# Two groups of modulation sums made beside the delta projections, and half a group in each merge round

## The reference

```
proj = rmsnorm(x) @ w_in                       # 12,560 columns
o1 = gated_delta_rule(silu(conv4(qkv)), ...)   # 8 heads of 128, chunks of 64 tokens
o2 = sliding_window_attention(...)             # 8 heads of 64
o3 = stick_breaking_attention(...)             # 4 heads of 128
merged = sum_i sigmoid(gates_i) * (o_i @ w_br_i)
h = x + merged @ w_o
h = h + cross_attention(rmsnorm(h), mem)
h = h + (silu(gate) * val) @ w_down            # gate, val = conv3(rmsnorm(h) @ w_up)
```

```
mod = silu(c) @ mod_w + mod_b                  # [2048] @ [2048, 12288]
sh1, sc1, g1, sh2, sc2, g2 = split(mod, 6)
h = rms_norm(x) * (1 + sc1) + sh1
a, gt = split(h @ conv_w_in + conv_b_in, 2);  u = a * sigmoid(gt)
u = depthwise_conv(u, 31 taps);  u = silu(layer_norm(u)) @ conv_w_out + conv_b_out
x = x + (1 + g1) * u
h = rms_norm(x) * (1 + sc2) + sh2
x = x + (1 + g2) * (square(relu(h @ mlp_w1)) @ mlp_w2)
```

## Time and profile before

| | us |
|---|---|
| median of 3 runs | 2745.66 (2744.92 to 2746.29) |
| the profiled execution's own time | 2738.4 |
| its span, first to last instruction | 2736.8 |
| TensorE busy | 2660.2 (97%) |
| VectorE busy | 1836.4 (67%) |
| ScalarE busy | 1184.8 (43%) |
| mean granted TensorE clock | 0.988 of full speed |

### The profile page before, as it was taken

One profiled execution on the slowest core, in us unless ns is written; L12 is line 12 of the kernel. 1 busy time (PEld: TensorE's weight loads), 2 busy tenths in 40 slices (PEclk: granted clock), 3 DMA queues, 4 the chain that ended last, 5 costly groups with the idle time before them and its releaser, 6 DMA issues.

```text
span 2736.8 us, 46369 instructions
## 1 busy us (share of the span) xinstructions
PE 2660.2 (97%) x18056; PEld 2472.7 (90%) x18056; DVE 1836.4 (67%) x2116; ACT 1184.8 (43%) x1443; POOL 80.4 (3%) x172
## 2 busy tenths in 40 slices
PE   7999999999999998999999989998989999999998
PEld 6999998999998887998899878897889898898997
DVE  4675647788778877776577646998665555555554
ACT  5544426533334455554344452115454334343342
POOL 1000000000010000000000000000000000000000
PEclk9999999999999999999999999999999999999999
DMA  5633435888989875776677644442555665656654
GB/s 185 178 116 101 131 96 194 306 292 303 331 310 317 289 258 191 267 238 226 192 262 241 223 130 131 146 154 93 185 157 185 194 183 188 192 181 191 187 184 153
DMA packets 269373, 553.10 MB, mean 202 GB/s; under 512 B 17026, under 2 KB 54963, under 8 KB 267955
## 3 DMA queue, kind: packets, MB, share of 16 engines
q1 hardware_dynamic: 249698, 442.06, 49.8%
q0 software_dynamic: 18720, 102.77, 11.2%
q10 hardware_dynamic: 816, 6.29, 0.6%
HBM read 548.96 MB, written 2.10 MB: 201 GB/s over the span
## 4 chain that ended last, share of the span: by engine, by line
PE 86%; DVE 8%; ACT 2%; issue 1%; DMA 1%; SPq 0%; POOLq 0%; ACTq 0%; DVEq 0%
PE sums L617 78%; DVE cv L1632 3%; PE small L1487 3%; DVE w_lo L573 1%; DMA mod_raw<-in_mod_w_dram 1%; DVE mod_acc L1177 1%; ACT w_hi L564 1%; PE small L1189 1%; PE small L1608 1%; PE sums L1223 0%; PE small L738 0%; SPq L1686 0%; PE small L1500 0%; PE small L1494 0%; PE small L698 0%
## 5 line engine op out<-in xcount | busy, mean ns | idle before, releaser
L573 DVE TENSOR_TENSOR w_lo<-raw,w_hi 128x1024 fp32r<-128x1024 f32 x790 | 960.1, 1222 | 740.9 <-ACT w_hi L564 738.3
L564 ACT ACTIVATE w_hi<-raw 128x1024 fp32r<-128x1024 f32 x790 | 834.3, 1059 | 1372.5 <-PE sums L617 1193.1
L617 PE MATMUL sums<-x_hi,w_hi 128*128 128x256 f32 x3728 | 1069.0, 287 | 9.1 <-DVE w_lo L573 3.9
L617 PE MATMUL sums<-x_lo,w_hi 128*128 128x256 f32 x3728 | 1060.5, 284 | 0.0
L617 PE MATMUL sums<-x_hi,w_lo 128*128 128x256 f32 x3728 | 1060.2, 284 | 0.0
L617 PEld LDWEIGHTS sums<-x_hi,w_hi 128*128 128x128 f32 x3728 | 720.8, 193 | 13.8 <-issue 8.5
L617 PEld LDWEIGHTS sums<-x_lo,w_hi 128*128 128x128 f32 x3728 | 721.2, 193 | 1.1 <-issue 0.7
L617 PEld LDWEIGHTS sums<-x_hi,w_lo 128*128 128x128 f32 x3728 | 720.7, 193 | 0.0
L617 PE MATMUL sums<-w_hi,y_hi 128*128 128x512 f32 x928 | 364.2, 392 | 7.0 <-issue 6.4
L617 PE MATMUL sums<-w_lo,y_hi 128*128 128x512 f32 x928 | 363.0, 391 | 0.0
L617 PE MATMUL sums<-w_hi,y_lo 128*128 128x512 f32 x928 | 362.8, 391 | 0.0
(11 more groups left out here) (352 smaller groups left out, 1970.1 us busy)
## 6 DMA issues: line engine op xcount, KB each, us to landing
raw<-in_mlp_w_dram SPq DMA_DIRECT2D x256, 512.0 KB, 3.8
raw<-in_w_in_dram SPq DMA_DIRECT2D x198, 512.0 KB, 4.4
mod_raw<-in_mod_w_dram POOLq DMA_DIRECT2D x128, 768.0 KB, 6.1
raw<-in_w_up_dram SPq DMA_DIRECT2D x128, 512.0 KB, 4.4
raw<-in_w_down_dram SPq DMA_DIRECT2D x64, 512.0 KB, 4.4
raw<-in_conv_w_in_dram SPq DMA_DIRECT2D x128, 256.0 KB, 3.2
raw<-in_w_o_dram SPq DMA_DIRECT2D x32, 512.0 KB, 5.6
raw<-in_conv_w_out_dram SPq DMA_DIRECT2D x32, 512.0 KB, 4.3
```

The lines of the kernel that those rows point to most:

```text
L564: act.activation(w_hi[:, s.slot(k), :], raw[:, s.slot(k), :], ACT.Copy).then_inc(hi_ready, 1)
L573: dve.tensor_tensor(w_lo[:, s.slot(k), :], raw[:, s.slot(k), :], w_hi[:, s.slot(k), :].bitcast(F32), ALU.subtract).then_inc(lo_ready, 1)
L617: mm = pe.matmul(o, l, r, start=first and i == 0, stop=end and i + 1 == len(steps), skip_group_check=True)
```

## The change

Groups 0 and 1, 32 mod units, move out of the merge rounds into the second halves of delta chunks 1 to 7: 4, 4, 4, 5, 5, 5 and 5 units. `rest_units` spreads them over the last four units of a chunk, and where there are five, two stand behind the last. They have buffers of their own (`mod_first`, in the space of the residual `h`, and `acc_first` and `acc_second`, in that of `y_hi` and `y_lo`), and both sums are cleared in chunk 1. POOL's loads start when the first norm is scaled. Group 0's `mod_sum` comes ahead of the last unit before the second delta group and waits for the first group's `y_lo`; a wait for `mod_kept` stands between it and L1494's second turn. Group 1's `mod_sum` stands in `attention_pe`. Merge rounds then make half a group each (3, 3 and 2 units in the first three chunks), and sum it in rounds 1 and 3. The whole units of `conv_in` are now 0, 1, 2, 4, 5 and 6, so the split ones are 3 and 7, and the taps are spread differently.

```diff
-CV_WHOLE = 6
+CV_WHOLE = (0, 1, 2, 4, 5, 6)
...
         def mixer_pe(pe):
-            for g in range(2):
-                yield 7 if g == 0 else 5
-                yield from delta_pe(pe, g)
+            yield 7
+            yield from delta_pe(pe, 0)
+            yield 4
+            pe.wait_ge(y_split, 1)
+            mod_sum(pe, KT, acc=acc_first)
+            yield 1
+            pe.wait_ge(mod_kept, 1)
+            yield from delta_pe(pe, 1)
             yield 4
             yield from attention_pe(pe)
...
             ins.then_inc(win_twice, 1)
-            yield 1
+            mod_sum(pe, 2 * KT, acc=acc_second)
+            yield 1
+            pe.wait_ge(mod_kept, 2)
...
         def mixer_dve(dve, own):
-            for g in range(2):
-                yield 8 if g == 0 else 5
-                yield from delta_dve(dve, own, g)
+            yield 8
+            yield from delta_dve(dve, own, 0)
+            yield 3
+            mod_keep(dve, 0, 1)
+            yield 2
+            yield from delta_dve(dve, own, 1)
...
+            pool.wait_ge(norm_scaled, TT)
+            for m in range(EARLY * KT):
+                if m >= 2:
+                    pool.wait_ge(mod_used, m - 1)
+                q, kt = m // KT, m % KT
+                pool.dma_start(mod_first[m % 2][:, :], mod_w_2[0][kt * P:(kt + 1) * P, q * MOD_W:(q + 1) * MOD_W]).then_inc(
+                    mod_loaded[m % 2], 16)
...
-                    rest_units(dve, s, SLOTS + 4, s.size + SLOTS, beside=beside)
+                    n = 4 * g + m
+                    if n == 1:
+                        clear_mod(dve, acc_first)
+                        clear_mod(dve, acc_second)
+                    first = (0, 0, 4, 8, 12, 17, 22, 27, 32)
+                    rest_units(dve, s, SLOTS + 4, s.size + SLOTS,
+                               lambda j: mod_unit(dve, first[n] + j, (first[n] + j) % KT), first[n + 1] - first[n], beside)
...
-                clear_mod(dve)
-                kt = 0
-                for m, units in enumerate((5, 5, 4, 2, 0, 0)):
+                if i % 2 == 0:
+                    clear_mod(dve)
+                kt = 8 * (i % 2)
+                q = EARLY + i // 2
+                for m, units in enumerate((3, 3, 2, 0, 0, 0)):
...
-                    for k, taps_ahead in zip(range(*ahead(s)), (10, 20, 40, 50, 54, 57, 60, CV_B * TAPS)):
+                    for k, taps_ahead in zip(range(*ahead(s)), (8, 16, 24, 31, 39, 47, 55, CV_B * TAPS)):
```

More of the change, by code:

```diff
@@ L90, in is_whole @@
     def is_whole(self, u):
-        first, chunks, size, count = self.whole
-        return first <= u < first + chunks * size and (u - first) % size < count
+        first, chunks, size, which = self.whole
+        return first <= u < first + chunks * size and (u - first) % size in which
     def whole_ahead(self, u):
-        first, chunks, size, count = self.whole
+        first, chunks, size, which = self.whole
         d = min(max(u - first, 0), chunks * size)
-        return d // size * count + min(d % size, count)
+        return d // size * len(which) + sum(k < d % size for k in which)
 class Spot:
@@ L257, in build_program @@
             win_q = sb("win_q", [P, 4, T], scope=s)
+        with ExitStack() as s:
+            mod_first = [sb(f"mod_first{j}", [P, MOD_W], scope=s) for j in range(2)]
         h = sb("h", [P, TT, D])
@@ L813, in nf_split_dve @@
                     scaled(g + 1)
-                if u == NF_CONV and g < CV_WHOLE:
+                if u == NF_CONV and g in CV_WHOLE:
                     continue
@@ L828, in normed_ready @@
         def normed_ready(pe, u, g):
-            if u == NF_CONV and g < CV_WHOLE:
+            if u == NF_CONV and g in CV_WHOLE:
                 pe.wait_ge(nf_hi, NG * u + g + 1)
             else:
-                pe.wait_ge(nf_split, NF_SPLITS[u] + g + 1 - (CV_WHOLE if u == NF_CONV else 0))
+                pe.wait_ge(nf_split, NF_SPLITS[u] + g + 1 - (sum(k < g for k in CV_WHOLE) if u == NF_CONV else 0))
         def shift1(kt):
@@ L1128, in attention_dve @@
         def attention_dve(dve, own):
+            mod_keep(dve, 1, 2)
             yield 1
@@ L2145, in merge @@
                         beside.rest()
-                    rest_units(dve, s, *ahead(s), lambda j: mod_unit(dve, kt + j, kt + j, (i, KT)), units, beside)
+                    rest_units(dve, s, *ahead(s), lambda j: mod_unit(dve, q * KT + kt + j, kt + j), units, beside)
                     kt += units
@@ L2163, in merge @@
                                   ALU.subtract).then_inc(merged, 1)
-                mod_keep(dve, i, at(1, (i, 1)))
+                if i % 2:
+                    mod_keep(dve, q, q + 1)
             merge(0, beside)
-            with own.loop(4, 3, 1) as i:
+            for i in range(1, 4):
                 merge(i, None)
```

47 lines of the change are left out of this document (25 added, 22 removed).

## The result

The changed kernel takes 2765.22 us (median of 4 executions, 2763.72 to 2771.46), against 2745.97 for the kernel before on the same chip: 1.0072 times as long, 95% interval 1.0057 to 1.0088, which is 16 to 24 us more. I had said 2760.5, in a range of 2750 to 2775. The profiled execution took 2765.18. That is 26.8 more than the profiled one of before, which at 2738.4 was a short one: the kernel before has a median of 2746.2 over 32 executions. So a comparison of the two traces shows some 7 us more than the medians do; I come back to them.

What follows compares the result with a forecast made beforehand. TensorE's chain of matmuls was taken as the bound, busy 2660 of 2737 us. The terms summed to +14.8 on the profiled 2738.4, 2753.2; adding 7.3 to reach the median gave 2760.5, range 2750 to 2775.

Steps and rivals of the forecast that it cites:

- The bound, and the merges: Whole kernel: TensorE's matmul chain bounds it; work taken from merge rounds was hidden, so a round stays at 92.25 us.
- rival C: Delta stage: VectorE's idle time takes in the mod units, only savings remain, 2740.4 us; chance 0.10.
- Term 1: Delta chunks 1 to 3: bursts of mod units waiting for loads make taps and L1494 late, +4.0 us (0 to 5).
- Term 2: Delta chunk 4: mod units ahead of low_t and v_nat delay L1530 and L1487, +5.4 us (4.5 to 7).
- term 3: Delta chunks 5 and 6: two small waits behind mod units, +0.9 us (0.3 to 1.5).
- Term 4: Delta chunk 7: mod units and loads delay mod_keep, which releases the second L1494, +10.3 us (7.7 to 11.5).
- the sign of being wrong: Chunk 7: a short wait at mod_keep, where more than 7 us was expected, would show the prediction wrong.
- Term 5: mod_sum: two additions of 2.57 us leave merge rounds 0 and 2 and return in delta stage and attention, 0.
- I take 0, and up to 5: Half clock behind new long waits on TensorE: priced at 0 us, up to 5 for the range.
- Term 6: Attention and merge 0: waits at L1069 and at a projection go with fewer mod units, -3.5 us (-4 to 0).
- Term 7: conv_in: two w_lo waits and the half clock behind them go, VectorE limits the gain, -2.3 us (-3 to -0.5).
- Early w_lo (unit 3) and another spread of taps remove both: conv_in: moving unit 3's w_lo and the taps ends both 1.95 us waits and their half clock, 1.7 us each.

Runs made afterwards that it cites:

- tiny_units: The changed kernel with each of the 32 early mod units cut to 64 of 1536 columns, in load and on VectorE: 2748.0 us, ratio 1.0009.
- two_loads: The changed kernel with only the first two modulation weight loads, 30 left out, all VectorE work kept: 2761.0 us, ratio 1.0062.
- none_in_7: The changed kernel with no mod units in delta chunk 7, and 5, 5, 6, 5, 5, 6 in chunks 1 to 6: 2773.0 us, ratio 1.0105.
- keep_early: The changed kernel with group 0's mod_keep one step earlier on VectorE, behind mod unit 29 instead of 31: 2765.3 us, ratio 1.0076.
- conv_back: The changed kernel with its conv_in part undone (split units 6 and 7, old spread of taps): 2768.1 us, ratio 1.0078.
- conv_alone: The kernel before with only the conv_in part (split units 3 and 7, taps spread evenly): 2747.9 us, ratio 1.0014.
- conv_ordered: The kernel before with the conv_in part, sigmoid and gated product ahead of the next chunk's unit 3 in chunks 0 to 6: 2744.3 us, ratio 0.9994.
- conv_best: The kernel before with the conv_in part, products ahead of unit 3 in chunks 0 to 6 and of conv_out units 1 to 3 in the last: 2734.4 us.
- glu7_early: The kernel before with only conv_in's last chunk's sigmoid and gated product moved two units earlier: 2743.5 us, ratio 0.9993.
- conv_best2: conv_best with ScalarE's squares of chunk 5 ahead of the last three w_hi: 2735.3 us, ratio 0.9965 to the kernel before.

## Why the prediction was right

**The bound, and the merges (first part).** Right. Taking half the mod units out of a merge round left it at 92.2 us; rival C's premise, that the units sit in idle time, fell with tiny_units: they cost 17 us.

**Term 1, +4.0.** Measured 5.5 by 144.16 (4.4, and the 1.1 of the common start): 3.7 of waiting, close to the 4.0 (1.2 of it in two small steps ahead of L1494, at 114 and 117 us, where w_lo came late), and 1.8 of half clock in L1521. Its cause, loads late in bursts, is shown by two_loads. That a fifth unit in a burst costs more is shown by none_in_7.

**Term 2, +5.4; term 3, +0.9.** Measured 5.2 and 1.4, with the waits at low_t (1.9, predicted 1.7) and k_nat (2.4, predicted 2.7).

**Term 4, +10.3, with mod_sum 12.8.** Measured 13.1, but the way there was not the prediction's alone: it had TensorE wait for mod_keep for over 7 us, and the wait was 2.9, since mod_sum and one unit had run at half clock meanwhile. So the sign of being wrong that the prediction named, a short wait at mod_keep, came in part: its 7 and more us were 2.9. keep_early shows that this stretch alone would have held L1521 but for 2.6.

**Term 5, 0: mis-sized.** A mod_sum is 2.57 in the chain of waits where the full clock holds, and every place that it left or came to adds a chance of half clock. Where the two now stand they cost 4.3 in the changed kernel's attention, 5.9 in tiny_units', and 6.9 in tiny_units' chunk 7 with the wait of 2.0 in it. With the slow tail behind the second L1521 (24.2 to 27.4), which the prediction held possible and priced at nothing ("I take 0, and up to 5"), this is what the delta and attention part cost more than forecast, 31.6 against 25.7. One reason that it gave was a misread row: I took the 5.8 us that the chain of waits spends on VectorE ahead of 180.12 for TensorE's waiting. But the chain only follows what released L1487. TensorE was at work in that time; the window of chunk 4, columns as in the earlier trace rows:

```profile
152.00:200.00 48.00, 47.75 (x408) 47.34 (x407) 36.21 (x46) 18.11 (x20) 0.00 (x0) 1.00 0.39 112
```

So the row says nothing of the price of a wait. The Trainium skill ("TensorE: Matmul & The Clock Gate", Part 1) had an idle array fall to 1.2 GHz; behind the 3.5 us of chunk 7 the trace agrees, 0.50. Behind waits of 1.9 and 2.4 in chunk 4 the clock stayed at 1.00, and it also fell behind mod_sums with no wait ahead of them.

**Term 6, -3.5.** From L1002 to round 3's mod_sum the delay falls by 10.9 (by 7.8 in conv_back's trace, with slow stretches behind both mod_sums); 5.1 of it are two mod_sums less, 2.2 is L1069's wait, gone as predicted. The other 3.6 hold the wait of 1.5, and 1.5 by which the last of before's merge rounds and its mod_sum (93.50 and 2.84) were slower than the first.

**Term 7, -2.3: the wrong sign.** +4.5 to +4.7. The step that failed is "Early w_lo (unit 3) and another spread of taps remove both", with nothing set against it. TensorE's waits for w_lo did fall from two of 3.8 us together to one of 1.4, none with a half clock behind, and in the changed kernel and in conv_alone it gained 5.5 us from chunk 0 to chunk 3. But I gave the moved unit's w_lo a place and not its w_hi, which stands on ScalarE ahead of the sigmoid and waits there for TensorE. conv_ordered shows it for 3.6 of the loss, 2.8 to 3.8 by the first tap. The rest is read from the traces: TensorE's idle time ahead of its taps, with the half clock behind (19.42 for the 76 matmuls in place of 16.68).

**The sum.** Forecast +14.8, measured +19.3 by the medians and +26.8 between the traces. Against the traces, on which the terms were worked out, the sum is 12 short. Term 7 is 6.8 of that; the half clock in the first L1521, behind the second, and in and behind the attention's mod_sum is 6.7 (1.8, 3.2 and 1.7); the merges gave 2.2 more than forecast. That the time is off by 4.7 and not by 12 is partly luck: the 7.3 that I added to come from the profiled execution to the median happened to cover the rest.

Those 7.3 lie in before's profiled execution. Six kernels have the same code up to conv_in. What sets their traces apart there is how long TensorE ran at its half clock (summed from the granted clock, from 50 us to the place of 1530.88):

| us | before | conv_alone | conv_best | glu7_early | conv_best2 | conv_ordered |
|---|---|---|---|---|---|---|
| at half clock | 23.9 | 27.3 | 27.3 | 37.5 | 47.8 | 54.6 |
| later at 1530.88 | 0 | -1.6 | 0.0 | 5.7 | 7.2 | 11.0 |

Many of these stretches stand behind a mod_sum. Whether one falls slow changes from execution to execution; what decides it, no run here shows.

## What to carry to other kernels

Work that was hidden beside a saturated TensorE gave nothing back here when it was moved, and cost time where the new place has a chain through the same engine: before moving such work, list what stands behind it in order, on every engine that touches the moved unit, down to the ScalarE instruction that makes its first half. Price a new long wait on TensorE with the slow matmuls that may follow: behind the 3.5 us here they cost near 5 more (2.5 in mod_sum, 2.2 in the unit). Don't read an engine's idle time from the chain of waits, but from a view of the waits or of its own busy time. Set the granted clock of two traces side by side before explaining a difference of a few us between them. Where two stages of a pipeline are nearly balanced, look for the instruction at its seam (here a gated product behind others that nobody waits for): with that moved, the conv_in part turned from a loss of 4 us into a gain of 10.

## What was not expected of the hardware

- 24 instructions of one-column matmuls took 2.73 us, and the next 24, with no wait between, 5.18; the matmuls of 128x512 behind them took 0.63 in place of 0.39 us. In merge rounds a stretch at half clock followed 18 of 40 such runs, at a cost of 1.5 or 3.0 us, though TensorE had not waited.
- A wait of 3.5 us on TensorE was followed by 10 us at a granted clock of 0.50. Those of 1.9 us (L1557) and 2.4 us (L1514 behind k_nat) in chunk 4 were followed by 5 and more us at 1.00, but the same two waits in conv_back and in two_loads (1.9 and 2.0 us in both) each by some 3 us at half clock. The one of 2.2 us at the first L1521 was followed by some 3 us at half clock as well.
- Loads of 768 KB took 5.3 us in the median beside the delta projections and 5.2 in the later stages, against 6.1 before the change; the shortest was 4.3 and is 4.4 now.
